# Regrouping a differential attention's maps through DRAM, and starting its output projection with half of its features

## The reference

```python
def diff_attention(q1, q2, k1, k2, v, lam, bias_dist):      # blocks of 128 queries
        def probs(q, k):
            s = jnp.einsum('bqhd,bkhd->bhqk', q, k).astype(jnp.float32) * scale + bias
            s = jnp.where(causal, s, -jnp.inf)
            return jax.nn.softmax(s, axis=-1)

        a = probs(qa, k1) - lam * probs(qc, k2)
        return jnp.einsum('bhqk,bkhd->bqhd', a.astype(v.dtype), v)

def even_mixer(h, w_in, w_out, ...):
    o = diff_attention(q[..., 0, :], q[..., 1, :], k[..., 0, :], k[..., 1, :], v, lam, bias_dist)
    o = (rms_norm(o, subln_g) * (1.0 - lambda_init)).reshape(B, S, A_WIDTH)
    y = multi_scale_pool(u, pool_w, pool_scale)
    return jnp.concatenate([o, y], axis=-1) @ w_out
```

## Time and profile before

| | before |
|---|---|
| median of 3 runs | 2283.13 us (2282.74 to 2283.8) |
| the profiled execution | 2282.54 us |
| its span | 2280.8 us |
| granted TensorE clock, mean | 0.998 |
| PE, PEld busy | 99%, 81% |
| DVE, ACT, POOL busy | 56%, 39%, 1% |
| DMA | mean 114 GB/s |

### The profile page before, as it was taken

One profiled execution on the slowest core, in us unless ns is written; L12 is line 12 of the kernel. 1 busy time (PEld: TensorE's weight loads), 2 busy tenths in 40 slices (PEclk: granted clock), 3 DMA queues, 4 the chain that ended last, 5 costly groups with the idle time before them and its releaser, 6 DMA issues.

```text
span 2280.8 us, 28255 instructions
## 1 busy us (share of the span) xinstructions
PE 2265.3 (99%) x11178; PEld 1844.8 (81%) x11178; DVE 1280.7 (56%) x2115; ACT 883.8 (39%) x1487; POOL 13.9 (1%) x14
## 2 busy tenths in 40 slices
PE   9999999999999999999999999999999999999998
PEld 7777778878777888788898888888888888888887
DVE  5865655567656556566555544444755536444445
ACT  5444533344445344364343422322322335332233
POOL 0000000000000000200000000000000000000000
PEclk9999999999999999999999999999999999999999
DMA  5655443336644334224353232223222213322231
GB/s 177 176 164 167 141 128 99 100 105 185 175 139 155 97 102 137 81 85 137 102 155 123 94 101 93 92 95 100 93 93 94 92 38 102 97 97 93 93 99 58
DMA packets 122471, 259.64 MB, mean 114 GB/s; under 512 B 12479, under 2 KB 66367, under 8 KB 122212
## 3 DMA queue, kind: packets, MB, share of 16 engines
q1 hardware_dynamic: 122340, 257.84, 36.2%
HBM read 229.73 MB, written 24.13 MB: 111 GB/s over the span
## 4 chain that ended last, share of the span: by engine, by line
PE 97%; DVE 1%; ACT 1%; POOL 0%; issue 0%; DMA 0%; SPq 0%; POOLq 0%; DVEq 0%; ACTq 0%
PE ps L378 28%; PE ps L380 27%; PE ps L379 27%; PE ps L621 2%; PE ps L729 2%; PE ps L404 2%; PE ps L405 2%; PE ps L406 2%; PE ps L1576 1%; PE ps L1515 1%; PE ps L470 1%; ACT t_Tb L190 1%; POOL t_UP L178 0%; PE ps L1013 0%; PE ps L1011 0%; PE ps L1012 0%
## 5 line engine op out<-in xcount | busy, mean ns | idle before, releaser
L378 PE MATMUL ps<-t_P0H,t_whi 128*128 128x512 f32 x1664 | 668.8, 402 | 1.7 <-DVE t_P0L L184 1.7
L380 PE MATMUL ps<-t_P0H,t_wlo 128*128 128x512 f32 x1664 | 656.3, 394 | 0.0
L379 PE MATMUL ps<-t_P0L,t_whi 128*128 128x512 f32 x1664 | 655.2, 394 | 0.0
L190 ACT ACTIVATE t_whi<-t_raw 128x1024 fp32r<-128x1024 f32 (+3 forms) x395 | 404.7, 1028 | 403.9 <-PE ps L380 330.1
L181 DVE TENSOR_TENSOR t_wlo<-t_raw,t_whi 128x1024 fp32r<-128x1024 f32 (+3 forms) x394 | 467.9, 1188 | 40.1 <-PE ps L406 19.9
L378 PEld LDWEIGHTS ps<-t_P0H,t_whi 128*128 128x128 f32 x1664 | 313.5, 188 | 95.5 <-issue 23.3
L380 PEld LDWEIGHTS ps<-t_P0H,t_wlo 128*128 128x128 f32 x1664 | 312.9, 188 | 72.8
L379 PEld LDWEIGHTS ps<-t_P0L,t_whi 128*128 128x128 f32 x1664 | 313.3, 188 | 71.4 <-issue 2.4
L378 PE MATMUL ps<-t_P1H,t_whi 128*128 128x512 f32 (+1 forms) x932 | 361.2, 388 | 0.3 <-DVE t_P1L L181 0.3
L379 PE MATMUL ps<-t_P1L,t_whi 128*128 128x512 f32 (+1 forms) x932 | 359.5, 386 | 0.0
L380 PE MATMUL ps<-t_P1H,t_wlo 128*128 128x512 f32 (+1 forms) x916 | 355.5, 388 | 0.0
(11 more groups left out here) (242 smaller groups left out, 2319.2 us busy)
## 6 DMA issues: line engine op xcount, KB each, us to landing
t_raw<-in_wts SPq DMA_DIRECT2D x362, 512.0 KB, 3.5
far<-t_Tb SPq DMA_DIRECT2D x26, 384.0 KB, 3.0
far<-t_Tb SPq DMA_DIRECT2D x16, 512.0 KB, 3.3
t_PTX<-far SPq DMA_DIRECT2D x64, 96.0 KB, 2.5
t_raw<-in_wts SPq DMA_DIRECT2D x16, 384.0 KB, 3.0
t_QKV<-far SPq DMA_DIRECT2D x32, 128.0 KB, 3.2
t_raw<-in_wts SPq DMA_DIRECT2D x13, 256.0 KB, 2.9
t_PTX<-far SPq DMA_DIRECT2D x24, 128.0 KB, 4.1
```

Source lines behind the costliest of these rows:

```text
L190: return lambda e: e.activation(o, a, f, **k)
L378: e.matmul(bank[:, 0:N], wh, xh, start=first, stop=False)
L379: e.matmul(bank[:, 0:N], wh, xl, start=False, stop=False)
L380: return e.matmul(bank[:, 0:N], wl, xh, start=False, stop=end)
```

## The change

Three parts. The differential maps go the way of the first block: `norm` gets a branch for them in the `by_dma` path, and the combined map is written, regrouped and read back as a unit of three or four tiles; the transposes on PE and the copies on ACT go. The tiles for it are the three of the pooling's scratch `UP` (one for `blocks`, two for `grouped`) and the two of `PTb`, and the bank of `PTP` joins `SB`. The head norms are made head by head, by steps that each put off the next one: square, sums (in a bank of `SB`), root, reciprocal and diagonal, spread, scaling and split. Three output projections are begun with the pooling's features 4 to 7 and completed with 0 to 3 once these are there; the other five follow. The fill is spread at 92/26 instead of 90/42.

```diff
             if by_dma:
                 far, ffree = blocks.take()
                 kh = u["cols"] // 128
+                if "nlam" in u:
+                    (t0, _), (t1, _) = u["T"]
+                    f4 = far[:, 0:128 * kh].rearrange("p (j k b) -> p k j b", j=4, b=32)
+                    z = [op(AC, act(t0[:, o1:o1 + n], t0[:, o1:o1 + n], ACT.Copy, scale=s[:, 12 + k:13 + k]), r)
+                         for k, (o1, n, _) in enumerate(parts)]
+                    r = op(DV, ts(s[:, 14:16], s[:, 14:16], u["nlam"], None, ALU.mult), r)
+
+                    def cut3(t, b):
+                        return t[:, 128 * b:128 * b + 128].rearrange("p (j b) -> p j b", j=4)
+
+                    o = [op(DV, stt(f4[:, b], cut3(t1, b), s[:, 14 + k:15 + k], cut3(t0, b), ALU.mult, ALU.add),
+                            z[k], r, ffree)
+                         for k, (o1, n, _) in enumerate(parts) for b in range(o1 // 128, (o1 + n) // 128)]
+                    TB.give(t0, o[-1])
+                    TB.give(t1, o[-1])
+                    STT.give(s, o[-1])
+                    u["far"], u["tiles"] = (far, o), kh
+                    return
...
-    hs = {}
+    blocks.idle = [(UP[:, 0, 0:512], pooled[0])]
+    grouped.idle = [(UP[:, i, 0:512], pooled[0]) for i in (1, 2)]
+    turned.idle = list(PTS.idle)
+    SB.idle += PTP.idle
+    PTP.idle = []
 
     def head_done(u, banks, p):
         h = u["pair"]
         o = op(DV, lambda e: e.tensor_copy(qE[:, h, :], banks[0]), p)
+        got = {}
 
         def square():
-            t, sq = tmp_act_square(qE[:, h, :], o)
-
-            def rest():
-                hs[h] = stats(t, sq, out=lp[:, 136 + 4 * h:140 + 4 * h], inv=1.0 / 128)
-                TMP.give(t, hs[h])
-
-            later(rest, 2)
+            got["sq"] = tmp_act_square(qE[:, h, :], o)
+            later(sums, 2)
+
+        def sums():
+            t, sq = got["sq"]
+            c = slice(136 + 4 * h, 140 + 4 * h)
+            r = stats(t, sq, out=lp[:, c], inv=1.0 / 128, B=SB)
+            TMP.give(t, r)
+            got["root"] = op(AC, act(lp[:, c], lp[:, c], ACT.Sqrt), r)
+            later(column)
+
+        def column():
+            c = slice(152 + 4 * h, 156 + 4 * h)
+            r = op(DV, lambda e: e.reciprocal(lp[:, c], lp[:, 136 + 4 * h:140 + 4 * h]), got["root"])
+            got["diag"] = diagonal(lp[:, c], r)
+            later(row)
+
+        def row():
+            got["row"] = spread_it(got["diag"], dst=kE[:, h, :], B=SB)
+            later(scale)
+
+        def scale():
+            q = op(DV, stt(qE[:, h, :], qE[:, h, :], lp[:, 134:135], kE[:, h, :], ALU.mult, ALU.mult), got["row"], lamt)
+            split_into(P1, h, qE[:, h, :], q)
 
         later(square)
         return [o]
 
-    def even_main():
-        yield from attention(eun, head_done, late_values=True)
+    drive(attention(eun, head_done, by_dma=True), fill_E(), 92, 26, lead=2)
+    xo = residual(1.0, lambda m, o: norm_tile(m, o, "xa0", P0, sqa), P0)
+    early = [gemm_fm(P1, Weight(chunk("ab_w_out", 0, halves(0), halves(128 * m, 1))),
+                     [(k, k) for k in (4, 5, 6, 7, 0, 1, 2, 3)], xo(m)) for m in range(3)]
+    for g in early:
         for _ in range(4):
+            next(g)
             flush()
-            yield
-        a = op(AC, act(lp[:, 136:152], lp[:, 136:152], ACT.Sqrt), *[hs[h] for h in range(4)])
...
-    drive(even_main(), fill_E(), 90, 42, lead=2)
     drain()
+    assert all(P1.tok)
+    for g in early:
+        run(g)
+    for m in range(3, 8):
+        run(gemm_fm(P1, Weight(chunk("ab_w_out", 0, halves(0), halves(128 * m, 1))), parts8(), xo(m)))
+    row_end()
...
-    run(mixed("ab_w_out", 0, halves(0), 1.0, "xa0", P1))
-    row_end()
-
     blocks.idle = [(E3[:, 9, :], None)]
     grouped.idle = [(E3[:, i, :], None) for i in (10, 11)]
-    turned.idle = [(ap, f) for ap, f in PTS.idle]
-    SB.idle += PTP.idle
-    PTP.idle = []
```

More of the change, by code:

```diff
@@ L1450, in even_main @@
             flush()
-            yield
-        a = op(AC, act(lp[:, 136:152], lp[:, 136:152], ACT.Sqrt), *[hs[h] for h in range(4)])
-        yield
-        a = op(DV, lambda e: e.reciprocal(lp[:, 152:168], lp[:, 136:152]), a)
-        d = diagonal(lp[:, 152:156], a)
-        yield
-        for h in range(4):
-            s = spread_it(d, dst=kE[:, h, :], B=SB)
-            if h < 3:
-                d = diagonal(lp[:, 156 + 4 * h:160 + 4 * h], a)
-            yield
-            o = op(DV, stt(qE[:, h, :], qE[:, h, :], lp[:, 134:135], kE[:, h, :], ALU.mult, ALU.mult), s, lamt)
-            flush()
-            split_into(P1, h, qE[:, h, :], o)
-            yield
```

## The result

The changed kernel takes **2288.4 us** (median of 16 executions, 2284.36 to 2291.24); before takes 2283.15 us in 16 executions beside it. The ratio is 1.0022, with a 95% interval of 1.0015 to 1.0028: it is slower by some 5 us, where 6.7 us less were forecast. The profiled execution took 2289.93 us with a span of 2288.1 us, against 2282.54 and 2280.8 before. DVE is busy for 56% of the span as before, PE for 99%.

A forecast was written before the change was run, and what follows sets the result against it. PE, busy for 99% of the span, was taken as the bound. Savings of 12.3 us less costs of 5.6 gave 6.7 us off the 2283.1 us median: 2276.5 us said, forecast case 2274 to 2279, range 2271 to 2284.5.

The forecast's parts named there:

- part 7: Head norms by steps: PE waits of 0.9 us for head 0, 0.1 for heads 1 and 2, 0.3 for head 3.
- Part 8: End of the stage: PE waits 2.0 us for the last values, and low clock behind it adds 0.8 us.
- part 6: Start of the stage: the third query projection waits 1.1 us, then 0.4 once more; 1.0 us taken, bounds 0 and 3.
- part 5: DVE's added work in mid-stream: DVE goes from 75% to 91% busy, costing 0.5 us, bounds 0 and 8.
- Parts 1 to 3: Savings on PE: transposes 4.3 us, matmul changes 1.0, waits and low clock 6.1, third scores bank 0.9; 12.3 in all.
- The change of kind between matmuls: Values and scores stand next to each other, so 12 slower first fill matmuls go: 1.0 us saved.
- Part 4: The maps' route through DRAM in mid-stream: a chain of about 12.2 us within 14.9, costed at nothing, 2.7 us of cover.
- The slow outcome by SP's queue: Rival: writes, reads and weights queue late on SP; with 4 us of delay 16 us more, 2292 us; chance 0.11.
- The clock: Low clock behind the wait for the last values at the stage's end: 0.8 us, half of the earlier 1.5.
- The table loads: Rival: each ACT table load holds ACT up for twice its 1.28 us, half of which shows: 2279 us; chance 0.05.
- All of it hides: Rival: values come without a wait and DVE keeps up, only 1.2 us of costs left: 2272 us; chance 0.17.
- DVE becomes the bound: Rival: DVE is 0.4 us short in each unit, 5 us more than forecast: 2281.5 us; chance 0.25.

The follow-up runs named there:

- no_dram: The changed kernel without the self-attention's write to DRAM and its reads, maps coming out in another order: 2286.89 us.
- aligned_9: three_moves with nine early output projections (features 4 to 6) handed out behind the fill and twelve left behind the attention: 2278.99 us.
- pe_turns: The changed kernel with the maps transposed on PE again, values in before's order and 90 fill steps for 28 places: 2282.54 us.
- no_roots: The changed kernel with a copy in place of the four square roots of the head norms: 2287.79 us.
- row_later: The changed kernel with each head's spread put one step further behind the column step: 2283.31 us.
- sums_later: The changed kernel with each head's sums put one step further behind the square: 2285.97 us.
- three_moves: The changed kernel with the moves of row_later, sums_later and last_finish together: 2282.21 us.
- three_no_dram: three_moves without the self-attention's write to DRAM and its reads: 2275.77 us.
- aligned_9_row: aligned_9 with head 0's spread alone one step earlier, where the changed kernel has it: 2280.51 us.
- last_finish: The changed kernel with the end of the fill's last key/value projection moved behind the attention, ahead of the early output projections: 2286.67 us.
- whole_parts: The changed kernel with the maps combined by one DVE instruction per part, not one per 128 columns: 2283.43 us.
- aligned_9_whole: aligned_9 with the maps combined by one DVE instruction per part: 2276.47 us.

## Why the prediction was wrong

By its own terms, the forecast for T was -6.7 us and +6.7 came. The waits make 6.0 us of the 13.4, the clock 5.7, PE's work 1.8. The step that failed is part 7, the waits at the heads' sums and spreads: 1.3 us were put down for them and 5.6 came, because its list of what stands ahead on DVE was short by one unit's normalisation and it had no term for the sums. Part 8 was short by 1.4 us, part 6 by 0.8, part 5 had 0.5 that didn't come; and each of the longer waits can bring a low stretch of the clock, of which one was priced.

**Parts 1 to 3, the savings.** Right in kind, too large in size. No transposes are left on PE, and the waits and the low clock of the earlier trace rows went, 6.1 us. The rest was put at 6.2 us and is 4.4. By the starts in the timelines, 40 transposes took 3.8 us, not 4.3, and the scores gained 0.8 of 0.9. The change of kind between matmuls was taken as a saving of 1.0 us; it is 1.1 to 1.4 us in the key and value fill, but by steps the sums and spreads stand among other matmuls, and by the starts in the six executions at full clock the sums, spreads, values and 512-column projections take 0.8 to 2.3 us more in all. That wasn't resolved further.

**Part 4, the route in mid-stream: right.** No values wait in mid-stream in after, no transpose there waits for a read, and no_dram leaves W as it is. The slow outcome by SP's queue didn't happen; a slow outcome by another way did. The rule of the Trainium skill that spoke for PE's transposes ("VectorE: DVE Perf Modes", section "Rules for kernel authors") costs here, where PE is the full engine, 3.7 to 3.8 us of it for 40 tiles. The best kernel that goes through DRAM takes 2279.0 us (aligned_9), the one that transposes on PE 2282.5 (pe_turns). These two differ in the order of their steps as well, and no run transposes on PE in aligned_9's order with the end covered, so how much of the 3.5 us is the route's isn't shown.

Two sums of the prediction don't come out as written, and neither matters here. The terms of part 4's chain add up to 11.6 us; with the 0.6 us of the transpose they are the 12.2 given. Part 7's 6.1 against 5.3 us is a wait of 0.8, not 0.9.

**Part 5, DVE.** DVE was expected to be at 85 to 92% in the key and value part. It is at 32.83 us of 40 from 995 to 1035 us:

```profile
995.00:1035.00 40.00, 39.15 (x286) 34.29 (x286) 32.83 (x91) 24.91 (x47) 0.00 (x0) 0.96 0.54 163
```

82%, and no fill step waited for a low part. The half microsecond of mid-stream waits didn't come. The failure is elsewhere: I asked whether DVE has room over a unit, and not how far behind it is at the moment when a head's step asks for it.

**Part 6, the start: 1.8 us for 1.0.** The walk itself gave 1.1 + 0.4 and 1.0 was taken; 0.66 and 1.19 came.

**Part 7, the head norms: the largest miss.** Head 0's spread was walked at 0.9 us and waits 3.5. From the end of the fill ahead of the sums, the walk gave PE 5.3 us of work and DVE 6.1. In after PE, then DVE, with the lines between left out:

```profile
986.16 0.83 PE L747 MATMUL ps<-t_PTb,t_E 128*128 128x128 f32 x6
...
995.29 1.33 PE L470 MATMUL ps<-t_TMP,t_ones 128*128 128x512 f32 x2 [3.50 <-DVE t_TMP L175]
```

```profile
986.33 0.18 DVE L664 RECIPROCAL t_ST<-t_ST 128x4 f32<-128x4 f32 x1 [0.89 <-ACT t_Tb L190]
...
987.56 1.14 DVE L184 SCALAR_TENSOR_TENSOR t_UP<-t_Tb,t_ST 128x128 f32<-128x128 f32 x4 [0.79 <-ACT t_Tb L190]
988.61 0.57 DVE L599 STREAM_TRANSPOSE t_PTb<-t_UP 128x384 f32<-128x384 f32 x1
...
994.54 0.69 DVE L175 TENSOR_TENSOR t_TMP<-t_ident,t_lam 128x512 f32<-128x512 f32 x1
```

PE has 9.1 - 3.5 = 5.6 us of work, as walked. DVE takes 9.1 us from 986.16 to the diagonal's end. Of these, 6.1 are what the walk lists (one transpose, four maxima, two low parts, an eviction as two value tiles, the column step) and 0.6 are stands for ACT. The other 2.4, until 988.61, are the normalisation of the unit just made: a reciprocal, a wait for ACT's scaled copy and four multiply-adds. Part 5 counts it for every unit, and part 7 leaves it out. no_roots shows that the wait is DVE's order, and that the table loads hide but for 0.3 us, as the prediction said. The spreads of heads 1 to 3 don't wait. For the sums the prediction has no term, and head 2's wait 2.1 us:

```profile
1034.34 0.72 ACT L190 ACTIVATE t_Tb<-t_Tb,t_ST 128x512 f32<-128x512 f32 x1 [3.95 <-DVE t_ST L187]
...
1035.14 0.72 ACT L190 ACTIVATE t_Tb<-t_Tb,t_ST 128x512 f32<-128x512 f32 x1
...
1035.86 0.62 ACT L190 ACTIVATE t_TMP<-t_E 128x512 f32<-128x512 f32 x1
```

The square stands on ACT behind the exponentials of the last unit, and these wait 3.95 us for maxima that DVE begins 2.7 us after the scores' end. The walk doesn't look at what stands ahead of the square. row_later and sums_later show both as matters of place.

**Part 8, the end: 2.0 us forecast, 3.4 came, and by another way.** The walk took the transpose to wait for the reads. In after it stood behind the low part, the value tiles and a split that wait for PE's last value projection. I had written that `finish` comes at the end of every projection, and left its DVE work out at the one place where the fill runs out. The chain that I did walk was there as well: three_moves uncovers it at 3.6 us, and three_no_dram takes it away. "They can't cover it", of the early projections, was right of their place and is what aligned_9 mends.

**The clock: 0.8 us forecast, 6.5 in the profiled execution.** I priced a low stretch behind one wait. There are three, of 1.5, 3.0 and 2.4 us by their lengths and clocks, and by the mean clocks of after's executions how much of it comes differs from one execution to the next.

**The rivals.** The table loads, which had 0.05, hide but for 0.3 us at head 0 (no_roots). "All of it hides", 2272 us, needed a cover at the end that the change doesn't have. "DVE becomes the bound", 2281.5, named the engine; its mechanism of a full unit didn't come, its arrears did. The case on the slow side was given 0.11 with SP as its only way. A case "the waits in order at the heads' steps" should have stood beside it, since the change puts two such steps for each head, sums and spread, into the queue of an engine with 1% of idle time.

## What to carry to other kernels

A share of busy time doesn't say whether an engine can serve a queue in order. For every step that a full engine must take in order, list what stands ahead of its producer on the producer's own engine, waits and all, and count the work between; one `later` more (row_later) was worth 5 us here. Where two causes meet at one place, as the order and the transfer before the last values, taking one away shows nothing: take both, and then put work there, since what covers a wait must stand ahead of it in the queue. And a wait on PE can bring a stretch at low clock behind it, by an amount that differs from one execution to the next, so compare medians of many; on the other hand the engine waited for catches up meanwhile, so the wait's own length isn't its price either (2.4 us put back cost 1.5 in aligned_9_row).

## What the runs showed of the hardware that was not expected

- The low clock behind a wait isn't a fixed cost. Two kernels with W of 10.8 and 10.4 us had 6.5 us and none of it in their profiled executions. Behind its wait of 3.2 us aligned_9_row has a granted clock of 0.74 from 995 to 1000 us, and behind one of 3.6 us three_moves a few matmuls at 0.43 us; in whole_parts nothing of the kind follows one of 3.4. The three kernels with no wait over 1.4 us repeat within 1.9 us (aligned_9, eleven executions), 1.7 (aligned_9_whole, seven) and 1.1 (three_no_dram, five), after within 6.9 (sixteen), last_finish within 4.8 (eleven).
- Waits for DVE aren't additive: 2.4 us put back at one place took 2.7 us away from others.
- DVE served its queue strictly in order. In no_dram, where the last map is combined by 1039.4 us and needs no transfer, its transpose starts at 1048.33, and DVE stands for 2.8 us meanwhile behind a low part that waits for PE. In after it stands for 5.9 us at that place; the last read is issued by 1043.5 us and the reads there take up to 3.2 us to land, so its transpose can have been ready for the last 1.3 us at least. ACT stood for 3.95 us before an exponential, at its end with the square's input ready for 1.3 us. That ACT's and DVE's queues are strict is what the Trainium skill says ("TensorE: Matmul & The Clock Gate", section "Architectural detail: the array is 16× 32×32, not 1× 128×128"), and these traces agree.
